# Transposed squares in a delta-rule inverse: a second product or a transpose of the copied square

## The chip, the cores and the metric

One core of one Trainium2 chip runs the whole kernel. The metric is the device time of one execution in microseconds, as the median of several runs. The core has TensorE (PE; its weight loads are listed as PEld), VectorE (DVE), ScalarE (ACT), GpSimd (POOL) and the DMA queues, one of them fed by SyncE (SP). They work side by side and wait for each other with semaphores.

## The reference, cut to what matters

The model is a two-layer trunk over 512 latent and 256 context tokens of width 1024. Each layer has three token mixers side by side (grouped attention, neighbourhood attention, a gated delta rule in both directions), a merge and an MLP. The change lies in the delta rule, where a 64 x 64 strictly triangular matrix per chunk and head is inverted by repeated squaring:

```
nil = jnp.where(strict, -jnp.einsum('nbhid,nbhjd->nbhij', kb, kc) * decay, 0.0)
tinv = jnp.eye(CHUNK, dtype=F32) + nil
power = nil
for _ in range(int(math.log2(CHUNK)) - 1):     # 5 times
    power = power @ power
    tinv = tinv + tinv @ power
w_v = tinv @ (vc * bc[..., None])
k_cd = tinv @ (kb * jnp.exp(gc)[..., None])
```

After this a scan over the chunks updates the state with w_v and k_cd. All of it is float32.

## The kernel before, in words

The program is written out by engine: `block.tensor`, `block.vector`, `block.scalar`, `block.gpsimd` and a SyncE part each hold one list of instructions, in program order, with waits between them. There is no planner; the order of the lines is the order on each engine.

**The delta stage.** Two chunks of 64 tokens stand on the diagonal of one 128 x 128 matrix, so a tile of 128 tokens is one step: `for s in range(TT)`, 6 steps per layer, 12 in all. Each step treats two directions (`d`, forward and backward, on different token tiles) and four heads (`h`), which lie beside each other in a 128 x 512 buffer. A step consists of the head (decays, L591 to L597; the matrix A, built by DVE up to L1264; its transpose AT, four PE transposes per direction, L604), five squaring iterations (`i`), then k_cd (L641) and two state updates (L656 to L674).

**One squaring iteration, before.** The stationary operand of a PE product is used transposed, so the kernel keeps the power and its transpose. `power(d, i)` names four buffers: `src`, `srcT` (the power and its transpose that come in) and `dst`, `dstT` (those that go out). They swap from one iteration to the next. For each direction PE multiplies, head by head, the square into columns 0 to 511 of a PSUM tile (L615) and, for i < 4, the transposed square into columns 512 to 1023 (L617). ACT copies the first half into `dst` (L953), DVE the second into `dstT` (L1275). Then PE multiplies `dst` with the transposed inverse `xbuf` (L626), and DVE adds the product to `xbuf` (L1279). The transposed square is needed only by the squares of the next iteration; at i = 4 there is none.

**PSUM.** There are four PSUM tiles `PS` of 128 x 1024. `take` hands them out in turn and waits until the tile's previous user has been read twice (its free count goes up by two). `read(...)` is that full count as a wait, `read_first(...)` the count less one, `full(...)` waits for PE's mark that the tile is filled, and `pair(...)` is the tile. `pe_done` is PE's own signal, with a named mark for each point.

**Between the iterations of layer 0.** For the first 20 iterations of layer 0 (steps 0 to 3, all five `i`), PE does one block of the modulation after each: `modulation_columns` (L407, one transpose) and `modulation` (L397, products with w_mod, four slots of 512 KB). The slots come through the ring `wring` of three, filled by SyncE's queue in the order of `plan` (L816); a slot's transfer is issued when PE has read the slot three before it. Steps 4 and 5 of layer 0 and all of layer 1 have nothing between the iterations.

**At the end of a step** POOL overwrites `pbuf` (L1517) once the last square (i = 4) is filled, and the head of the next step begins when the last state update of this one is read.

Of the kernel before, what the change touches and what calls it, by code (L numbers as in the profile page):

```python
# [21 lines left out]
P = 128  # L22
# [8 lines left out]
A_H, A_KV, B_H, C_H = 8, 2, 8, 4  # L31
# [71 lines left out]
def program(nc, a, out, x_store, skew, bias_rows, book):  # L103
    book["final"] = book.get("final", False)
    with ExitStack() as ctx:
# [35 lines left out]
        ident, ones, blk, rot = (cst[:, c:c + P] for c in (C_ID, C_ONE, C_BLK, C_ROT))  # L141
# [82 lines left out]
        act_done, dve_done, pool_done, pe_done = sig("act_done"), sig("dve_done"), sig("pool_done"), sig("pe_done")  # L224
# [14 lines left out]
        def full(*key):  # L239
            n = book.get(("ps",) + key, 0) if book["final"] else 0  # L240
            return ps_full[n % 4], n // 4 + 1
# [4 lines left out]
        def pair(*key):  # L246
            return PS[book.get(("ps",) + key, 0) % 4]
# [5 lines left out]
        def read(*key):  # L253
            n = book.get(("ps",) + key, 0) if book["final"] else 0
            return ps_free[n % 4], 2 * (n // 4 + 1)

        def read_first(*key):

            sem, n = read(*key)
            return sem, n - 1  # L260
# [111 lines left out]
        def _(pe):  # L372
            turn["n"] = 0
            mm, tr = nc.tensor.matmul, nc.tensor.transpose
# [144 lines left out]
            for l in range(DEPTH):  # L519
                if l == 0:  # L520

                    for t in range(TT):
                        pe.wait_ge(*x_in[t].at())
                        ps = take(pe, "x", t)
                        for k in range(KC):
                            last = tr(ps[:, k * P:k * P + P], r(S0 + 1024 * t, 1024)[:, k * P:k * P + P], ident)
# [15 lines left out]
                for p in range(15):  # L542
# [9 lines left out]
                    if p == 2:  # L552
                        pe.wait_ge(*read("baT", l))
                        ps = take(pe, "ba", l)
                        for t in range(TT):
                            last = tr(ps[:, 16 * t:16 * t + 16], baT[0:16, t * P:t * P + P], ident[0:16, 0:16])
                        last.then_inc(*filled("ba", l))
                    if p == 4:

                        pe.wait_ge(*dve_done.at("g", l))  # L560
                        ps = take(pe, "gc", l)
                        for t in range(TT):
# [4 lines left out]
                            for c in range(2):  # L567
                                last = mm(ps[:, b + 16 + 8 * c:b + 24 + 8 * c],
                                          blk[:, 64 * c:64 * c + 1].to_broadcast([P, P]), gt[:, t, :],
                                          start=True, stop=True)  # L570
                        last.then_inc(*filled("gc", l))
                    if p >= 3 and c_order[p - 3] < 8:
# [3 lines left out]
                        ps = take(pe, "css", l, j)  # L576
# [8 lines left out]
                for s in range(TT):  # L585
# [23 lines left out]
                    for i in range(5):  # L609
                        for d in range(2):  # L610
                            src, srcT, dst, dstT = power(d, i)
                            pe.wait_ge(*(read("pw", l, s, d, i - 1) if i else read("AT", l, s, d)))
                            ps = take(pe, "pw", l, s, d, i)
                            for h in range(C_H):
                                last = mm(ps[:, h * P:h * P + P], srcT[:, h, :], src[:, h, :], start=True, stop=True)  # L615
                                if i < 4:
                                    last = mm(ps[:, 512 + h * P:512 + h * P + P], src[:, h, :], srcT[:, h, :],  # L617
                                              start=True, stop=True)
                            last.then_inc(*filled("pw", l, s, d, i))
                        for d in range(2):  # L620
                            src, srcT, dst, dstT = power(d, i)
                            pe.wait_ge(*read("pw", l, s, d, i))
                            pe.wait_ge(*(read("X", l, s, d, i - 1) if i else read("AT", l, s, d)))
                            ps = take(pe, "X", l, s, d, i)
                            for h in range(C_H):
                                last = mm(ps[:, h * P:h * P + P], dst[:, h, :], xbuf[d][:, h, :], start=True, stop=True)  # L626
                            last.then_inc(*filled("X", l, s, d, i))
                        if l == 0:

                            if turned:  # L630
                                modulation_columns(*turned)
                            turned = next(filler, None)
                            if turned:
                                modulation(*turned)
# [421 lines left out]
        def _(dve):  # L1056
# [98 lines left out]
            for l in range(DEPTH):  # L1155
# [88 lines left out]
                for s in range(TT):  # L1244
                    for d in range(2):
                        t = tiles[d][s]
                        dve.wait_ge(*read_first("bc", l, s, d))
                        if s:
                            dve.wait_ge(*full("kcd", l, s - 1, d))
                        V.tensor_tensor(wbuf[d], pair("bc", l, s, d)[:, 0:512].rearrange("p (h n) -> p h n", h=C_H),  # L1250
                                        along(gcs[:, t, 4 * d:4 * d + 4]), ALU.subtract)\
                            .then_inc(*free("bc", l, s, d, by=1))
                        dve.wait_ge(*act_done.at("W", l, s, d))
                        dve.wait_ge(*full("G", l, s, d))
                        if s:
                            dve.wait_ge(*full("so", l, 2 * s - 1, d))
                        ps = pair("G", l, s, d)
                        V.tensor_tensor(flat(pbuf[d]), ps[:, 0:512], flat(wbuf[d]), ALU.mult)\
                            .then_inc(*free("G", l, s, d, by=1))
                        V.tensor_tensor(flat(aqbuf[d]), ps[:, 512:1024], flat(wbuf[d]), ALU.mult)\  # L1260
                            .then_inc(*free("G", l, s, d, by=1))
                        dve.wait_ge(*read("G", l, s, d))
                        dve.wait_ge(*pool_done.at("MB", l, s, d))
                        V.tensor_tensor(pbuf[d], pbuf[d], p2buf[d], ALU.mult).then_inc(*dve_done.mark("A", l, s, d))  # L1264
                    for d in range(2):
                        dve.wait_ge(*full("AT", l, s, d))
                        ps = pair("AT", l, s, d)
                        V.tensor_copy(flat(tbuf[d]), ps[:, 0:512]).then_inc(*free("AT", l, s, d, by=1))
                        V.tensor_tensor(xbuf[d], ps[:, 0:512].rearrange("p (h n) -> p h n", h=C_H), over_heads(ident),  # L1269
                                        ALU.add).then_inc(*free("AT", l, s, d, by=1))  # L1270
                    for i in range(5):
                        if i < 4:
                            for d in range(2):
                                dve.wait_ge(*full("pw", l, s, d, i))
                                V.tensor_copy(flat(power(d, i)[3]), pair("pw", l, s, d, i)[:, 512:1024])\  # L1275
                                    .then_inc(*free("pw", l, s, d, i, by=1))
                        for d in range(2):
                            dve.wait_ge(*full("X", l, s, d, i))
                            V.tensor_tensor(flat(xbuf[d]), pair("X", l, s, d, i)[:, 0:512], flat(xbuf[d]), ALU.add)\  # L1279
                                .then_inc(*free("X", l, s, d, i))  # L1280
                        if l == 0:
                            if turned:
                                modulation_columns(*turned)
                            turned = next(filler, None)
                            if turned:
                                modulation(*turned)
                    for c in range(2):
                        for d in range(2):
                            t, cc, n = tiles[d][s], (c if d == 0 else 1 - c), 2 * s + c
                            lo = 64 * cc  # L1290
                            ps = pair("so", l, n, d)
                            dve.wait_ge(*full("so", l, n, d))
                            if want_out(l, t):
                                o = Otok[lo:lo + 64, t, :]
                                if (t, cc) in seen:
                                    V.tensor_tensor(o, ps[lo:lo + 64, 512:1024], o, ALU.add).then_inc(*free("so", l, n, d, by=1))
                                else:
                                    V.tensor_copy(o, ps[lo:lo + 64, 512:1024]).then_inc(*free("so", l, n, d, by=1))
                                seen.add((t, cc))
                            dve.wait_ge(*pool_done.at("Sdec", l, n, d))  # L1300
                            S1 = state[:, (n + 1) % 2, 4 * d:4 * d + 4, :].rearrange("p a b -> p (a b)")
                            V.tensor_tensor(S1, ps[:, 0:512], S1, ALU.add)\
                                .then_inc(*free("so", l, n, d, by=1 if want_out(l, t) else 2))
# [338 lines left out]
```

## Time and profile before

| | |
|---|---|
| median of 3 runs | 3793.74 us (3784.53 to 3796.07) |
| profiled execution | 3801.55 us |
| its span on the core | 3799.7 us |
| its mean granted TensorE clock | 0.936 |
| TensorE busy | 3390.5 us (89%) |
| VectorE / ScalarE / GpSimd busy | 35% / 27% / 28% |
| squaring iterations (L615, L617, L626) busy on PE | 204.5, 171.4 and 126.8 us |

A span is from the first to the last instruction. Busy time counts the union of an engine's instructions; PE's overlap each other, so the mean duration of one is longer than the distance between two. One fp32 product shows as two MATMUL instructions, one fp32 transpose as one. "Granted clock" is the share of TensorE's full speed: 1.00 is 2.4 GHz, 0.50 is 1.2 GHz. In brackets behind an instruction stands how long its engine sat idle before it and whose work ended that.

### The profile page before, as it was taken

Reading aid. Unit: us, or ns where it says so; the run is one execution under the profiler, and the core shown is the slowest. Engines: PE = TensorE matmul, PEld = TensorE weight load, DVE = VectorE, ACT = ScalarE, POOL = GpSimd, SP = SyncE. Lnnn points to the kernel's source line nnn. Section 1 sums busy time; section 2 is a strip of 40 time slices with the busy share of each in tenths; the row PEclk is TensorE's granted clock in tenths of the full one; section 3 lists DMA queues with packets and bytes.
Section 4 is the critical chain, followed back from the end, with each engine's and each line's share of the span. In section 5 each row is a group of like instructions: output and inputs, shape, how many; then the busy total and the mean of one; then the engine's idle time right before and its main releaser. Section 6 shows DMA issues by size and latency. Waiting matters only on the chain.

```text
span 3799.7 us, 49641 instructions
## 1 busy us (share of the span) xinstructions
PE 3390.5 (89%) x21115; PEld 2809.3 (74%) x21115; DVE 1338.5 (35%) x1789; ACT 1014.4 (27%) x1614; POOL 1058.9 (28%) x679
## 2 busy tenths in 40 slices
PE   5977777989988999979999979799989989989997
PEld 3857777977766777858888858688977766658886
DVE  3672232412455111242222257544313552232222
ACT  2431111222354111232122133322222541133223
POOL 3232122232111111233223231333233022244443
PEclk6888899999999999989999988899999999989998
DMA  5213333011000222212222211000021013323331
GB/s 163 78 27 112 112 112 112 1 50 53 25 8 37 59 60 61 75 35 62 67 61 62 67 61 39 1 1 1 1 72 53 4 51 89 86 76 97 94 95 61
DMA packets 302570, 226.16 MB, mean 60 GB/s; under 512 B 16720, under 2 KB 275216, under 8 KB 301712
## 3 DMA queue, kind: packets, MB, share of 16 engines
q1 hardware_dynamic: 298992, 207.69, 18.6%
q0 software_dynamic: 3360, 15.29, 1.2%
q8 instruction: 169, 2.77, 0.3%
q14 instruction: 49, 0.40, 0.0%
HBM read 214.56 MB, written 9.36 MB: 59 GB/s over the span
## 4 chain that ended last, share of the span: by engine, by line
PE 81%; DVE 8%; DMA 3%; issue 3%; ACT 3%; POOL 1%; SPq 0%; ACTq 0%; POOLq 0%; DVEq 0%
PE ps L385 17%; PE ps L386 16%; PE ps L387 16%; PE ps L721 5%; PE ps L615 4%; PE ps L626 3%; DMA wring<-in_w_mod 3%; PE ps L617 3%; PE ps L465 2%; DVE stat L1100 1%; PE ps L486 1%; PE ps L669 1%; PE ps L512 1%; PE ps L656 1%; PE ps L503 1%
## 5 line engine op out<-in xcount | busy, mean ns | idle before, releaser
L385 PE MATMUL ps<-hh,wh 128*128 128x512 f32 (+1 forms) x2592 | 950.2, 367 | 106.9 <-DVE hl L1079 79.0
L1438 POOL TENSOR_TENSOR wl<-wring,wh 128x1024 fp32r<-128x1024 f32 x264 | 643.8, 2442 | 1379.4 <-ACT wh L867 1379.3
L386 PE MATMUL ps<-hl,wh 128*128 128x512 f32 (+1 forms) x2592 | 919.0, 355 | 0.0
L387 PE MATMUL ps<-hh,wl 128*128 128x512 f32 (+1 forms) x2592 | 917.7, 354 | 0.0
L385 PEld LDWEIGHTS ps<-hh,wh 128*128 128x128 f32 x2592 | 499.7, 193 | 202.8 <-issue 62.4
L386 PEld LDWEIGHTS ps<-hl,wh 128*128 128x128 f32 x2592 | 500.9, 193 | 74.0 <-issue 9.6
L387 PEld LDWEIGHTS ps<-hh,wl 128*128 128x128 f32 x2592 | 499.7, 193 | 67.6
L867 ACT ACTIVATE wh<-wring 128x1024 fp32r<-128x1024 f32 x264 | 277.6, 1054 | 909.4 <-DMA wring<-in_w_in 462.0
L386 PE MATMUL ps<-fl,wh 128*128 128x512 f32 (+1 forms) x768 | 274.8, 358 | 0.0
L387 PE MATMUL ps<-fh,wl 128*128 128x512 f32 (+1 forms) x768 | 274.5, 357 | 0.0
L385 PE MATMUL ps<-fh,wh 128*128 128x512 f32 (+1 forms) x768 | 274.3, 357 | 0.0
L1373 DVE SCALAR_TENSOR_TENSOR R<-ps,modcs,R 128x512 f32<-128x512 f32 x216 | 136.4, 659 | 389.7 <-PE ps L387 388.7
L721 PE MATMUL ps<-R,wring 128*128 128x512 f32 (+1 forms) x576 | 214.0, 521 | 0.0
L615 PE MATMUL ps<-R 128*128 128x128 f32 x960 | 204.5, 315 | 4.1 <-DVE R L1269 3.7
L1357 DVE TENSOR_TENSOR R<-ps,R 128x768 f32<-128x768 f32 (+1 forms) x48 | 39.6, 825 | 448.8 <-ACT R L1024 443.0
L1387 DVE TENSOR_TENSOR R<-R 128x768 f32<-128x768 f32 (+1 forms) x64 | 52.8, 826 | 367.0 <-ACT R L1041 367.0
L953 ACT ACTIVATE R<-ps 128x512 f32<-128x512 f32 x120 | 71.6, 597 | 401.1 <-PE ps L617 341.4
L615 PEld LDWEIGHTS ps<-R 128*128 128x128 f32 x960 | 167.4, 227 | 12.2 <-DVE R L1269 7.9
L617 PE MATMUL ps<-R 128*128 128x128 f32 x768 | 171.4, 310 | 0.0
L721 PEld LDWEIGHTS ps<-R,wring 128*128 128x128 f32 x576 | 107.5, 190 | 86.1 <-issue 80.5
L385 PEld LDWEIGHTS ps<-fh,wh 128*128 128x128 f32 x768 | 144.7, 188 | 23.7
L386 PEld LDWEIGHTS ps<-fl,wh 128*128 128x128 f32 x768 | 144.5, 188 | 23.3
(220 smaller groups left out, 4666.9 us busy)
## 6 DMA issues: line engine op xcount, KB each, us to landing
wring<-in_w_ffn SPq DMA_DIRECT2D x128, 512.0 KB, 4.0
wring<-in_w_in SPq DMA_DIRECT2D x116, 512.0 KB, 3.9
wring<-in_w_mod SPq DMA_DIRECT2D x96, 512.0 KB, 4.8
wring<-in_w_branch SPq DMA_DIRECT2D x48, 256.0 KB, 4.3
wring<-in_w_out SPq DMA_DIRECT2D x16, 512.0 KB, 4.0
x_store<-R POOLq DMA_DIRECT2D x2, 3072.0 KB, 9.6
R<-x_store POOLq DMA_DIRECT2D x2, 3072.0 KB, 10.8
R<-in_x SPq DMA_DIRECT2D x4, 512.0 KB, 7.5
```

What stands on the lines that cost most here:

```text
L385: mm(ps[:, t0:t1], ahk, rh[:, k, t0:t1], start=(k == 0), stop=False)
L386: mm(ps[:, t0:t1], ahk, rl[:, k, t0:t1], start=False, stop=False)
L387: last = mm(ps[:, t0:t1], alk, rh[:, k, t0:t1], start=False, stop=(k == kn - 1))
L465: last = mm(ps[u][:, c0:c0 + n1 - n0], q[lo:lo + HD, t * P:t * P + P], k[lo:lo + HD, n0:n1], start=True, stop=True)
L615: last = mm(ps[:, h * P:h * P + P], srcT[:, h, :], src[:, h, :], start=True, stop=True)
L617: last = mm(ps[:, 512 + h * P:512 + h * P + P], src[:, h, :], srcT[:, h, :], start=True, stop=True)
L626: last = mm(ps[:, h * P:h * P + P], dst[:, h, :], xbuf[d][:, h, :], start=True, stop=True)
L721: last = mm(ps[:, t0:t1], w[:, k, :], (oA, oB, oC)[x % 3][:, k, t0:t1], start=(k == 0), stop=(k == 3))
L867: A(slot_view(wh, n % NSPL, *slot), w, ACT.Copy).then_inc(*act_done.mark("whi", *slot))
L953: A(flat(power(d, i)[2]), pair("pw", l, s, d, i)[:, 0:512], ACT.Copy)\
L1373: V.scalar_tensor_tensor(out=xT[:, j, t0:t1], in0=pair(*key)[:, t0:t1], scalar=modc[:, gate + j, c:c + 1], in1=xT[:, j, t0:t1], op0=ALU.mu ...
L1438: G.tensor_tensor(slot_view(wl, n % NSPL, l, name, i), w, slot_view(wh, n % NSPL, l, name, i).bitcast(F32), ALU.subtract)\
```

## The change

PE no longer multiplies the transposed square (L617). Instead it waits until ACT has copied the square into `dst` (the first of the tile's two reads), transposes `dst` head by head into the same columns 512 to 1023 of the same PSUM tile, and marks that as `pwT`. DVE's copy into `dstT` waits for this mark, and DVE now goes direction by direction: transposed copy and X sum of direction 0, then those of direction 1. i = 4 is as before on PE and ACT. In this excerpt "..." stands for unchanged lines.

```diff
@@ PE: squares
                             for h in range(C_H):
                                 last = mm(ps[:, h * P:h * P + P], srcT[:, h, :], src[:, h, :], start=True, stop=True)
-                                if i < 4:
-                                    last = mm(ps[:, 512 + h * P:512 + h * P + P], src[:, h, :], srcT[:, h, :],
-                                              start=True, stop=True)
                             last.then_inc(*filled("pw", l, s, d, i))
                         for d in range(2):
                             src, srcT, dst, dstT = power(d, i)
-                            pe.wait_ge(*read("pw", l, s, d, i))
+                            if i < 4:
+
+                                pe.wait_ge(*read_first("pw", l, s, d, i))
+                                for h in range(C_H):
+                                    last = tr(pair("pw", l, s, d, i)[:, 512 + h * P:512 + h * P + P], dst[:, h, :], ident)
+                                last.then_inc(*pe_done.mark("pwT", l, s, d, i))
+                            else:
+                                pe.wait_ge(*read("pw", l, s, d, i))
                             pe.wait_ge(*(read("X", l, s, d, i - 1) if i else read("AT", l, s, d)))
...
@@ DVE: copies and sums
                     for i in range(5):
-                        if i < 4:
-                            for d in range(2):
-                                dve.wait_ge(*full("pw", l, s, d, i))
+                        for d in range(2):
+                            if i < 4:
+                                dve.wait_ge(*pe_done.at("pwT", l, s, d, i))
                                 V.tensor_copy(flat(power(d, i)[3]), pair("pw", l, s, d, i)[:, 512:1024])\
                                     .then_inc(*free("pw", l, s, d, i, by=1))
-                        for d in range(2):
                             dve.wait_ge(*full("X", l, s, d, i))
```

## Rows read from the trace of the kernel before

**Rows 1.** The page: span, and TensorE's busy time.
```profile
span 3799.7 us, 49641 instructions
PE 3390.5 (89%) x21115; PEld 2809.3 (74%) x21115; DVE 1338.5 (35%) x1789; ACT 1014.4 (27%) x1614; POOL 1058.9 (28%) x679
```

**Rows 2.** The page: the chain that ended last, by engine and by line.
```profile
PE 81%; DVE 8%; DMA 3%; issue 3%; ACT 3%; POOL 1%; SPq 0%; ACTq 0%; POOLq 0%; DVEq 0%
PE ps L385 17%; PE ps L386 16%; PE ps L387 16%; PE ps L721 5%; PE ps L615 4%; PE ps L626 3%; DMA wring<-in_w_mod 3%; PE ps L617 3%; PE ps L465 2%; DVE stat L1100 1%; PE ps L486 1%; PE ps L669 1%; PE ps L512 1%; PE ps L656 1%; PE ps L503 1%
```

**Rows 3.** Groups by line and shape: busy us, mean ns | idle before.
```profile
L615 PE MATMUL ps<-R 128*128 128x128 f32 x960 | 204.5, 315 | 4.1 <-DVE R L1269 3.7
```

**Rows 4.** Order of time, layer 1: start, us, engine, line, count.
```profile
2657.16 0.39 PE L615 MATMUL ps<-R 128*128 128x128 f32 x2
...
2660.74 2.10 PE L626 MATMUL ps<-R 128*128 128x128 f32 x16
2660.94 0.60 ACT L953 ACTIVATE R<-ps 128x512 f32<-128x512 f32 x1 [1.19 <-PE ps L617]
...
2662.68 0.39 PE L615 MATMUL ps<-R 128*128 128x128 f32 x2
```

**Rows 5.** Windows: stretch, length, busy by engine, clock, DMA share, GB/s.
```profile
2660.70:2666.20 5.50, 5.50 (x50) 5.42 (x50) 2.77 (x4) 1.19 (x2) 0.00 (x0) 1.00 0.00 0
2649.39:2653.80 4.41, 4.41 (x20) 4.41 (x21) 1.83 (x3) 0.60 (x1) 0.87 (x1) 0.50 0.00 0
```

**Rows 6.** Transposes: a group by line, and two runs in time.
```profile
L604 PE MATMUL ps<-cst,R 128*128 128x128 f32 x96 | 18.0, 317 | 43.9 <-DVE R L1264 43.9
...
14.46 1.09 PE L526 MATMUL ps<-cst,R 128*128 128x128 f32 x8 [0.24 <-DMA R<-in_ctx]
...
1103.84 1.53 PE L503 MATMUL ps<-cst,R 128*128 128x128 f32 x12
```

**Rows 7.** Order of time at i = 4, layer 1, step 4.
```profile
2673.71 1.95 PE L615 MATMUL ps<-R 128*128 128x128 f32 x16
...
2674.87 0.60 ACT L953 ACTIVATE R<-ps 128x512 f32<-128x512 f32 x1 [2.30 <-PE ps L615]
...
2675.52 2.05 PE L626 MATMUL ps<-R 128*128 128x128 f32 x16
```

**Rows 8.** Layer 0 around two modulations; the last two from the chain.
```profile
410.77 0.39 PE L626 MATMUL ps<-R 128*128 128x128 f32 x2
...
411.00 0.27 PE L407 MATMUL ps<-cst,mrow 128*128 128x128 f32 x1
...
411.20 1.52 PE L397 MATMUL ps<-wring,ccol 128*32 128x128 f32 x48
...
411.91 5.30 SPq L816 DMA_DIRECT2D wring<-in_w_mod  x4
...
415.69 1.08 PE L397 MATMUL ps<-wring,ccol 128*32 128x128 f32 x16 [2.98 <-DMA wring<-in_w_mod]
...
424.87 1.52 PE L397 MATMUL ps<-wring,ccol 128*32 128x128 f32 x48
...
481.47 1.94 PE ps L626 x16
...
492.45 1.94 PE ps L626 x16
```

**Rows 9.** Waits of TensorE, 279 to 760 us: total, times, longest.
```profile
PE ps L397 <- DMA wring<-in_w_mod: 62.6, 20, 4.5
```

**Rows 10.** Window over the steps with modulation; columns as in rows 5.
```profile
279.00:659.50 380.50, 301.90 (x3076) 275.46 (x3076) 109.13 (x193) 52.96 (x88) 80.89 (x73) 0.88 0.34 111
```

**Rows 11.** Windows over the first transposes, TensorE alone: busy, clock, DMA.
```profile
7.40:12.00 4.60, 4.60 (x22) 1.00 1.03 386
12.00:14.20 2.20, 2.20 (x20) 1.00 1.01 369
```

## The prediction

> **What bounds the kernel now.** I read the page's shares first, then the chain that ended last, the groups by line and shape, and last one squaring iteration in order of time. TensorE is busy for 3390.5 of 3799.7 us [rows 1]; the chain is TensorE for 81% of the span, and 4, 3 and 3% of it lie on L615, L617 and L626, the lines that the change touches [rows 2]. So what comes off TensorE here comes off the time, unless a wait takes its place.
>
> The stage is 12 steps (2 layers, 6 token tiles), each with 5 squaring iterations for two directions. The change touches i = 0 to 3, that is 48 iterations. In one of them in layer 1 [rows 4] TensorE issues 32 instructions for squares (L615, L617: each fp32 product shows as two) and 16 for X (L626). The squares start at 2657.16 and the next ones at 2662.68: 5.52 us for 48 instructions, while a window of 5.50 us shows TensorE busy throughout at granted clock 1.00 and VectorE for 2.77, ScalarE for 1.19 us [rows 5]. The durations of single instructions (315 ns in the mean) [rows 3] overlap and are not the price. The price is the distance of starts: 32 of them from 2657.16 to 2660.74, 0.112 each. 48 x 0.112 is 5.38; the remaining 0.14 lies inside L626 (16 instructions from 2660.74 to 2662.68, 1.94 instead of 1.79), where X of the second direction waits for the ScalarE copy that began at 2660.94.
>
> **The 16 squares that go.** Per iteration L617's 16 instructions go: 16 x 0.112 = 1.79 us.
>
> **The 8 transposes that come.** Transposes exist in the trace. A transpose is one instruction: L604 has 96, which is 12 steps x 2 directions x 4 heads [rows 6]. Spacing at full clock: 12 of them take 1.53 us with the last lasting 0.27, so (1.53 - 0.27)/11 = 0.115, a first restart included; 8 of L526 take 1.09, so 0.117 [rows 6].  I take 0.11. So 8 x 0.11 = 0.88. Bounds: 0.11 if they stream; 0.27 each (2.2 us) if each ran to its end before the next.
>
> **The new order and its waits.** Squares of direction 0 (8 instructions, 0.89), squares of 1 (to 1.79), then transposes of 0, which wait for ScalarE's copy of square 0. That hand-off is already in the trace, at i = 4, where there is no L617 [rows 7]: L615 starts at 2673.71, the copy at 2674.87 and takes 0.60, to 2675.47; L626 starts at 2675.52, 1.81 after the first square where 16 x 0.112 is 1.79. The wait costs 0.02 plus a restart of the array of about 0.1: 0.12, about the 0.14 that X of the second direction pays today and no longer will, because its transposes stand before it and come after the copy's end. In the new order, from the first square: transposes of 0 from 1.9 to 2.35, X of 0 to 3.25, transposes of 1 to 3.7 (copy 1 done at 1.99 + 0.60 = 2.6, no wait), X of 1 to 4.6. VectorE: transposed copy 0 from about 2.55 to 3.25, X sum 0 from 3.45 to 4.15, copy 1 from 4.15 to 4.85 (it is now queued behind X sum 0), X sum 1 from 4.85 to 5.5. The squares of direction 1 of the next iteration need copy 1 and come at 4.6 + 0.9 = 5.5: 0.6 us of slack, so VectorE hides; were that cover gone, TensorE would wait for it once per iteration. Squares of 0 need copy 0, done 1.3 us before. The PSUM tiles that the next iteration takes are free by the same times.
>
> New iteration: (16 + 16) x 0.112 + 0.88 + 0.12 = 4.58 against 5.52. Saving 0.94, in 32 iterations without anything between them (layer 0 steps 4 and 5, layer 1): 30.1 us. At each step's start the clock is low (granted 0.50 for 2649.39 to 2653.80 [rows 5]). If that low stretch keeps its length, what is removed is still paid at the full rate afterwards, so 0.94 stands for i = 0 too.
>
> **The 16 iterations with modulation between them** (layer 0, steps 0 to 3). Each ends in a product with w_mod through a ring of three slots; the fourth slot's transfer starts only when the first is read, and TensorE waits 3 us for it (2.98 [rows 8]; 62.6 us in 20 waits [rows 9]). That wait runs from the issue to the landing (411.91 to 415.69, 3.8 us), whatever the squares cost, and so it stays. The question is whether the other three slots are back in time. Four transfers are issued from 411.91 on, the last at 417.2, so by the same 3.8 us it lands at 421.0, 9.8 after the modulation began (411.20). The next begins at 424.87 today and at 423.9 with 0.94 less: covered. The quickest iteration took 11.0 (X groups at 481.47 and 492.45) and would take 10.0; the last to land is the third slot that it reads, which leaves it about 1 us. So 16 x 0.94 = 15.0. The modulation takes the PSUM tile that copy 1 frees; that is at 4.85, while it would start at 4.8: 0 to 0.2 us, taken 0.1, 1.6 in all. Then the clock: these iterations run at 0.88 granted over the stretch [rows 10], and their lengths go from 11.0 to 13.7 (411.20 to 424.87) by where the low stretches fall. The idle part, 3 us, becomes a larger share of a shorter iteration; I take 0.25 us more at the low level's cost for each, 4 us; either end is 1 us each way, 16 us.
>
> **The sum.** 30.1 + 15.0 - 1.6 - 4.0 = 39.5 us, say 40. The profiled execution took 3801.55 us around a span of 3799.7, so it would be 3762. It lies 7.8 above the median of the runs, 3793.74; from the median I get 3754.
>
> **Switching cost**, which no row shows for this pair of shapes exactly: there are four changes between full products and transposes in an iteration. From the last two L626 at 410.77 to the single transpose L407 at 411.00 are 0.23, no extra; from L407 to the narrow L397 takes 0.20, some 0.1 extra [rows 8]. Bounds 0 to 0.4 us an iteration, 19 us in all; I take 0, as both tiles here are 128 x 128 like L626 and L407.
>
> **A rule against it.** The first transposes of the kernel run with nothing else on TensorE: 22 instructions in the first 4.60 us (0.209 each, the 1.2 GHz level) and 20 in the next 2.20 us (0.110, the 2.4 GHz level) [rows 11] (the record of the clock begins later and its 1.00 says nothing of the first part). Transposes alone brought the clock up. The Trainium skill, "TensorE: Matmul & The Clock Gate", part 4 on PE-mode transpose, says that transpose mode does not count as busy for the clock and that one takes about 275 ns in a kernel's context. By that rule the changed iterations could fall to the lower level, the second rival below; the trace has the 273 ns as a duration and 0.11 as the spacing, and speaks against the first half.
>
> **Rivals.**
> 1. The ring takes back the gain of the 16 modulation iterations, by a later landing or a worse fall of the low stretches: only the 32 others pay, 30 us, 3764. For it: the margin of about 1 us in the quickest iteration. Against: the 3.9 us between landing and use in the iteration of rows 8.
> 2. Slower: the clock. The place is the squaring iterations, now with 0.88 of 4.58 us in transposes and a restart in each. If the 32 iterations ran at 1.2 GHz they would take 9.2 instead of 5.5 us, 32 x 3.6 = 117 slower, 3911. It decides from 80 us of additional low clock, each microsecond of which loses half of one. Against: rows 11, and attention, where 12 transposes stand in each unit at the full rate [rows 6].
> 3. Slower: transposes cost their own 0.273 in sequence: 8 x 0.16 = 1.3 more, 0.36 slower an iteration, 17 us, 3811. Against: the spacing of every row of transposes.
> 4. Each switch costs 0.1: 48 x 0.4 less, gain 21, 3773.
> 5. The ScalarE hand-off is exposed where the i = 4 row shows it hidden (0.60 + 0.2 us): 0.15 remains of an iteration, 7 us, 3787, no difference. The change would then not shorten the chain, only exchange products for a wait.
>
> **Chances.** Forecast 0.73, rival 1 0.12, rival 4 0.07, rival 5 0.03, rival 2 0.03, rival 3 0.02. 0.3%, 11.4 us, is what can be told from no change. Faster 0.92, same 0.03, slower 0.05. The range: at the good end 45 us and 10 from a better fall of the clock, 3738; at the other rival 4, 3773; I leave out rivals 2, 3 and 5. 3736 to 3774.
>
> **What would show it.** Right: L615 x960 and 384 transposes with spacing 0.11; X groups 4.6 us apart in layer 1 at granted 1.00; transposes of direction 0 starting 1.8 to 1.9 after the first square; VectorE's copy 1 ending before squares of direction 1; the modulation wait still 3 us; nothing else moved. Wrong: X groups further apart than 4.8; idle before L615 behind VectorE's copy; a granted clock under 0.90 in steps without modulation; waits on w_mod that grow by what the squares lose.

## The result and the profile after

The changed kernel took 3741.27 us in the median of 4 runs (3737.76 to 3744.07), the kernel before 3789.47 in 4 runs beside it: ratio 0.9871, 95% interval 0.9851 to 0.9892, so 48 us or 1.3% less. Timed again in five rounds (experiment 1) the ratio was 0.9847 (0.9826 to 0.9867), which is 1.5% or some 58 us; the two intervals overlap. Forecast were 3754 and a gain of 40.

The page of the profiled execution (3744.07 us), beside [rows 1, 2]: span, busy time, the chain by line (X is now L630, the transposes are L623).

```profile
span 3742.2 us, 48873 instructions
PE 3332.5 (89%) x20731; PEld 2755.2 (74%) x20731; DVE 1334.2 (36%) x1789; ACT 1014.9 (27%) x1614; POOL 1059.7 (28%) x679
PE 81%; DVE 8%; DMA 3%; issue 3%; ACT 3%; POOL 1%; SPq 0%; ACTq 0%; POOLq 0%; DVEq 0%
PE ps L385 17%; PE ps L386 17%; PE ps L387 17%; PE ps L725 6%; PE ps L615 4%; PE ps L630 3%; DMA wring<-in_w_mod 3%; DVE stat L1104 2%; PE ps L465 2%; PE ps L486 1%; PE ps L673 1%; PE ps L512 1%; PE ps L623 1%; PE ps L660 1%; PE ps L503 1%
```

TensorE has 384 instructions fewer (768 of L617 out, 384 transposes in) and 58.0 us less busy time, about what the span lost (57.5), and its share in the chain is still 81%. The other engines do what they did. L617's 3% of the chain have become 1% of L623.

One full iteration of layer 1 in order of time, beside [rows 4]: start, duration, engine, line, count; in brackets the idle time before.

```profile
2608.62 1.95 PE L615 MATMUL ps<-R 128*128 128x128 f32 x16
...
2609.71 0.60 ACT L957 ACTIVATE R<-ps 128x512 f32<-128x512 f32 x1 [3.58 <-PE ps L615]
2610.36 0.42 PEld L623 LDWEIGHTS ps<-cst,R 128*128 128x128 f32 x4
2610.41 0.61 PE L623 MATMUL ps<-cst,R 128*128 128x128 f32 x4
...
2610.86 1.06 PE L630 MATMUL ps<-R 128*128 128x128 f32 x8
2611.05 0.69 DVE L1279 COPY R<-ps 128x512 f32<-128x512 f32 x1 [1.47 <-PE ps L623]
...
2611.75 0.60 PE L623 MATMUL ps<-cst,R 128*128 128x128 f32 x4
2612.02 0.69 DVE L1282 TENSOR_TENSOR R<-ps,R 128x512 f32<-128x512 f32 x1 [0.27 <-PE ps L630]
...
2612.18 1.06 PE L630 MATMUL ps<-R 128*128 128x128 f32 x8
2612.63 0.68 DVE L1279 COPY R<-ps 128x512 f32<-128x512 f32 x1
...
2613.08 0.28 PE L615 MATMUL ps<-R 128*128 128x128 f32 x1
```

Read the starts: 2608.62 to 2613.08 is 4.46 us, where [rows 4] had 5.52. The squares take 1.79 (to 2610.41), four transposes 0.45 (to 2610.86, the last 0.11 of it their step to the product), and nowhere is there a gap. ScalarE's copy ends at 2610.31, the load of the first transpose begins 0.05 later, and the transpose itself starts 0.11 after the last square, as if there had been no wait. 1.06 is saved where the prediction had 0.94: of the 0.12 that it charged for the hand-off only about 0.01 came (0.45 for four transposes, where 4 x 0.109 is 0.44). VectorE's second copy ends at 2613.31; the squares of direction 1 that need it start at 2613.08 + 0.89 = 2613.97, the 0.6 us of slack that was forecast.

Three stretches, before and after: modulation iterations (layer 0, steps 0 to 3), the rest of layer 0's stage, layer 1's stage. Columns: stretch, length, busy time of PE, PEld, DVE, ACT, POOL, granted clock, DMA share, GB/s. First the kernel before:

```profile
279.06:659.46 380.40, 301.86 (x3076) 275.42 (x3076) 109.03 (x192) 52.96 (x88) 80.79 (x73) 0.88 0.34 111
659.46:750.79 91.33, 87.56 (x687) 83.68 (x688) 39.30 (x59) 19.84 (x34) 25.07 (x23) 0.94 0.00 1
2419.07:2739.06 319.99, 297.82 (x2334) 281.48 (x2335) 137.53 (x202) 72.80 (x122) 105.33 (x95) 0.95 0.00 1
```

and the changed one:

```profile
279.44:646.58 367.14, 290.33 (x2947) 263.05 (x2947) 107.47 (x192) 52.98 (x88) 80.81 (x73) 0.86 0.35 115
646.58:728.19 81.61, 77.73 (x623) 74.31 (x624) 38.53 (x59) 19.84 (x34) 25.09 (x23) 0.95 0.01 1
2392.50:2683.60 291.10, 269.40 (x2142) 254.85 (x2143) 135.29 (x202) 72.85 (x122) 105.45 (x95) 0.95 0.00 1
```

The stage gave 13.3 + 9.7 + 28.9 = 51.9 us; the remaining 5.6 of the two spans lie outside it, where nothing was changed, and are within the scatter of single executions (the five-round runs of before go from 3784 to 3805). Between the two layers' stages the first profile of the changed kernel took 1664.3 us and its second 1668.0, with no edit between them; the two of before took 1668.3 and 1668.1. The clock in the steps without modulation is 0.95 in both stretches (before: 0.94 and 0.95); in the modulation stretch it is 0.86 instead of 0.88.

### The profile page after: what moved, and what is told of

Read it like the earlier page. It is cut to its first block, busy times and chain, and to the rows that moved or that the text cites. A ratio compares the mean times of both kernels' runs of the same rounds, so it can differ in the third digit from the quotient of the medians.

```text
span 3742.2 us, 48873 instructions
## 1 busy us (share of the span) xinstructions
PE 3332.5 (89%) x20731; PEld 2755.2 (74%) x20731; DVE 1334.2 (36%) x1789; ACT 1014.9 (27%) x1614; POOL 1059.7 (28%) x679
## 3 DMA queue, kind: packets, MB, share of 16 engines
q1 hardware_dynamic: 298992, 207.69, 18.5%
## 4 chain that ended last, share of the span: by engine, by line
PE 81%; DVE 8%; DMA 3%; issue 3%; ACT 3%; POOL 1%; SPq 0%; ACTq 0%; POOLq 0%; DVEq 0%
PE ps L385 17%; PE ps L386 17%; PE ps L387 17%; PE ps L725 6%; PE ps L615 4%; PE ps L630 3%; DMA wring<-in_w_mod 3%; DVE stat L1104 2%; PE ps L465 2%; PE ps L486 1%; PE ps L673 1%; PE ps L512 1%; PE ps L623 1%; PE ps L660 1%; PE ps L503 1%
## 5 line engine op out<-in xcount | busy, mean ns | idle before, releaser
L385 PEld LDWEIGHTS ps<-hh,wh 128*128 128x128 f32 x2592 | 498.9, 192 | 202.9 <-issue 62.6
L387 PEld LDWEIGHTS ps<-fh,wl 128*128 128x128 f32 x768 | 144.4, 188 | 23.3
L615 PE MATMUL ps<-R 128*128 128x128 f32 x960 | 156.4, 331 | 3.7 <-DVE R L1273 3.1
L615 PEld LDWEIGHTS ps<-R 128*128 128x128 f32 x960 | 146.9, 242 | 13.1 <-DVE R L1273 7.6
```

Of the source, the lines that this page charges most:

```text
L385: mm(ps[:, t0:t1], ahk, rh[:, k, t0:t1], start=(k == 0), stop=False)
L387: last = mm(ps[:, t0:t1], alk, rh[:, k, t0:t1], start=False, stop=(k == kn - 1))
```

## The experiments

**1. The changed kernel again** (after_again), no edit.

> The changed kernel, unedited, for a narrower ratio and a second profile. Theory: an iteration without modulation again takes 4.46 us (32 product instructions at 0.112 and 8 transposes at 0.109), in all 32 places. What the first iteration of a step loses to the low clock (0.9 to 2.5 us in the first profile after, 1.1 to 3.0 before) should come out differently per step, but with the same sum of 12 to 15 us over the 8 steps without modulation, if the shorter step causes it; if it was the luck of one profile, nearer to the 19 us of before. Time 3737 to 3745, ratio 0.987 to 0.988.

Measured: 3738.96 us, ratio 0.9847 (0.9826 to 0.9867). All 24 iterations with i = 1 to 3 outside the modulation take 4.46 (one 4.54). The 8 first iterations of a step take 16.2 us more than 8 x 4.46; in the first profile after it was 14.0. So my bound of 12 to 15 was missed, and that loss scatters by some 2 us. The three stretches are 368.4, 83.0 and 291.9 us.

**2. The kernel before again** (before_again), no edit.

> The kernel before, unedited, for a second profile of the first iterations of the 8 steps without modulation. If its loss there is a property of the order of work, it is again 18 to 19 us (three steps of layer 1 at 8.5 us each); if it was chance, it lies anywhere between 12 and 19.

Measured: 3800.67 us in its one timed run; stretches 381.3, 90.8 and 320.0. The loss of the first iterations is 18.3, after 18.9 in the first profile. In layer 1 they repeat to 0.01 us: 8.56, 8.55, 8.54 in its first three steps the first time and 8.57, 8.55, 8.54 now; in layer 0 they differ (7.87 and 8.14, now 7.53 and 7.96). So for this kernel the loss is no luck of one profile. The changed kernel does not repeat in this way: its first iterations in the same three steps took 5.75, 6.97 and 5.97 in the first profile and 7.51, 6.25 and 5.60 in the second.

**3. Same products, squares first** (products_after). In the kernel before (VectorE's transposed copy then waits for `pwT`):

```diff
                             for h in range(C_H):
                                 last = mm(ps[:, h * P:h * P + P], srcT[:, h, :], src[:, h, :], start=True, stop=True)
-                                if i < 4:
-                                    last = mm(ps[:, 512 + h * P:512 + h * P + P], src[:, h, :], srcT[:, h, :],
-                                              start=True, stop=True)
                             last.then_inc(*filled("pw", l, s, d, i))
+                        for d in range(2 if i < 4 else 0):
+                            src, srcT, dst, dstT = power(d, i)
+                            for h in range(C_H):
+                                last = mm(pair("pw", l, s, d, i)[:, 512 + h * P:512 + h * P + P], src[:, h, :], srcT[:, h, :],
+                                          start=True, stop=True)
+                            last.then_inc(*pe_done.mark("pwT", l, s, d, i))
```

> The kernel before with one move: the squares of both directions first, then the transposed squares of both as products, then X; VectorE waits for the second group. Same instructions as before. Theory A (number of instructions): an iteration takes 48 x 0.112 = 5.37 us, so only the 0.14 restart of X in direction 1 goes; 48 x 0.14 = 7 us under before, 3783. Rival B (the order is what pays, since ScalarE's copy gets a head start): most of the 48 us come here too, 3745 to 3760. Rival C (nothing): the restart stays because X waits for both copies; 5.5, within 3 us of before.

Measured: ratio 1.0001 (0.9988 to 1.0014), 5.52 us an iteration. Theory A's 7 us did not come, and not the rival's 48 either: rival C was right. Its iteration (squares L615, second products L620, X L629):

```profile
2661.10 1.95 PE L615 MATMUL ps<-R 128*128 128x128 f32 x16
...
2662.20 0.60 ACT L956 ACTIVATE R<-ps 128x512 f32<-128x512 f32 x1 [4.46 <-PE ps L615]
2662.89 1.95 PE L620 MATMUL ps<-R 128*128 128x128 f32 x16
...
2663.99 0.69 DVE L1278 COPY R<-ps 128x512 f32<-128x512 f32 x1 [1.92 <-PE ps L620]
2664.73 2.05 PE L629 MATMUL ps<-R 128*128 128x128 f32 x16
```

ScalarE's copy ends at 2662.80, two microseconds before X. X starts at 2664.73, 0.05 after the end of VectorE's copy of the transposed square (2664.68). X waits with `read("pw", ...)`, the full count of the tile, that is for both copies, though it uses only ScalarE's. The same holds in the kernel before, and there the two end close together: ScalarE's at 2660.94 + 0.60 = 2661.54 [rows 4], VectorE's at 2660.94 + 0.69 = 2661.63:

```profile
2660.94 0.69 DVE L1275 COPY R<-ps 128x512 f32<-128x512 f32 x1 [1.09 <-PE ps L617]
```

I had put that wait down to ScalarE. It gave a new theory, F, and the next two kernels.

**4. Before, with X waiting for ScalarE alone** (x_waits_act). VectorE's copy now waits for ScalarE's, so that the first read of the tile is ScalarE's for certain:

```diff
-                            pe.wait_ge(*read("pw", l, s, d, i))
+                            pe.wait_ge(*(read_first("pw", l, s, d, i) if i < 4 else read("pw", l, s, d, i)))
...
-                                dve.wait_ge(*full("pw", l, s, d, i))
+                                dve.wait_ge(*read_first("pw", l, s, d, i))
```

> The kernel before with one wait changed: VectorE copies the transposed square only after ScalarE's copy of the square, and X waits for ScalarE's copy alone (in the kernel before X waits for both copies). Theory F: the 0.14 restart in each iteration of before came from VectorE's copy, which takes 0.69 us where ScalarE's takes 0.60, not from ScalarE's as the prediction had it; without it an iteration takes 5.37 to 5.45 instead of 5.52, 3 to 7 us faster than before. Rival: the restart comes from ScalarE's copy; 5.52 stays and the time is that of before.

Measured: ratio 0.9979 (0.9968 to 0.9989), 5.42 us an iteration (X groups of this kernel at 2650.09 and 2655.51). Theory F holds: 0.10 of the 0.14 was VectorE's copy. The gain in time, 0.2%, is small beside the scatter of single executions; the iteration's length is the surer sign.

```profile
2650.09 2.01 PE L626 MATMUL ps<-R 128*128 128x128 f32 x16
...
2655.51 2.01 PE L626 MATMUL ps<-R 128*128 128x128 f32 x16
```

**5. Both edits of 3 and 4** (products_after_x). VectorE's copy waits for the second group and for ScalarE's copy.

> products_after (squares of both directions, then both transposed squares as products, then X), and X waits for ScalarE's copy alone. products_after stayed at 5.52 us, because X waited there for VectorE's copies. Theory F: now every wait is over long before, so 48 x 0.112 = 5.37 us an iteration, 7 us under before, and the rest of the changed kernel's 1.06 us (0.92) belongs to the number of instructions alone. Rival: it stays at 5.52 again, and the restart is the cost of a switch from one group of products to the next.

Measured: ratio 0.9970 (0.9959 to 0.9981), 5.36 us an iteration. Squares, second products and X follow at 1.79, 1.79 and 1.78 us, no gap and no restart:

```profile
2643.01 1.95 PE L615 MATMUL ps<-R 128*128 128x128 f32 x16
2644.80 1.95 PE L620 MATMUL ps<-R 128*128 128x128 f32 x16
2646.59 1.95 PE L629 MATMUL ps<-R 128*128 128x128 f32 x16
2648.37 0.83 PE L615 MATMUL ps<-R 128*128 128x128 f32 x6
```

This is the kernel before without its wait: the same 48 product instructions. Against 5.52 the waits of before cost 0.16 an iteration. What the changed kernel has beyond it, 5.36 - 4.46 = 0.90, is products against transposes alone.

**6. Products in the transposes' place** (product_in_place). In the changed kernel:

```diff
-                                    last = tr(pair("pw", l, s, d, i)[:, 512 + h * P:512 + h * P + P], dst[:, h, :], ident)
+                                    last = mm(pair("pw", l, s, d, i)[:, 512 + h * P:512 + h * P + P], src[:, h, :], srcT[:, h, :],
+                                              start=True, stop=True)
```

> The changed kernel, but at the place of the four transposes stand the four products of the transposed square (8 instructions), behind the same wait for ScalarE's copy. Theory A: 48 x 0.112 = 5.37 plus a restart of 0.12 at the wait, since a product has two weight loads where a transpose has one: 5.49 us an iteration, 1 to 7 us under before. Rival B (the place and the wait matter, not what is done there): as fast as the changed kernel, 4.5 us.

Measured: ratio 0.9981 (0.9966 to 0.9997), 5.42 us an iteration. The rival, that place and wait are what pays, falls. My restart of 0.12 was too much again; it is 0.06, all in the first group after the wait:

```profile
2697.95 1.95 PE L615 MATMUL ps<-R 128*128 128x128 f32 x16
2699.74 1.12 PE L623 MATMUL ps<-R 128*128 128x128 f32 x8
2700.69 1.06 PE L631 MATMUL ps<-R 128*128 128x128 f32 x8
2701.58 1.06 PE L623 MATMUL ps<-R 128*128 128x128 f32 x8
2702.47 1.06 PE L631 MATMUL ps<-R 128*128 128x128 f32 x8
2703.37 0.39 PE L615 MATMUL ps<-R 128*128 128x128 f32 x2
```

The first L623 group takes 0.95 from its start to the next group, the second 0.89. The profiled execution took 3773.03, the shortest of this kernel's ten and 17 us under their median, so its stretch with modulation is not typical.

**7. Every transpose twice** (double_tr). In the changed kernel:

```diff
-                                for h in range(C_H):
+                                for h in list(range(C_H)) * 2:
                                     last = tr(pair("pw", l, s, d, i)[:, 512 + h * P:512 + h * P + P], dst[:, h, :], ident)
```

> The changed kernel with every transpose of a square done twice into the same columns. Theory A (a transpose costs its spacing): 8 x 0.109 = 0.87 more, 5.33 us an iteration, 48 x 0.87 = 42 over the changed kernel, near 3783. Rival D (a transpose costs its duration, 0.27): the spacing is 0.27 and 2.2 us come on top, 105 us. Rival E (transposes don't hold the clock up): the granted clock in steps without modulation falls from 0.95 towards 0.8 and the time is over 3800; by theory A it stays.

Measured: 3780.19 us, ratio 0.9963 (0.9944 to 0.9982), 41 above the changed kernel run beside it (42 expected). An iteration takes 5.34:

```profile
2641.82 1.95 PE L615 MATMUL ps<-R 128*128 128x128 f32 x16
2643.61 1.05 PE L623 MATMUL ps<-cst,R 128*128 128x128 f32 x8
2644.50 1.06 PE L630 MATMUL ps<-R 128*128 128x128 f32 x8
2645.39 1.04 PE L623 MATMUL ps<-cst,R 128*128 128x128 f32 x8
2646.26 1.06 PE L630 MATMUL ps<-R 128*128 128x128 f32 x8
2647.16 0.39 PE L615 MATMUL ps<-R 128*128 128x128 f32 x2
```

8 x 0.109 = 0.87 more: a transpose costs its spacing and not its duration. With a third of the iteration in transposes (1.75 of 5.34 us), TensorE spends 26.4 us of layer 1's stage at the low clock. The changed kernel has 26.4 and 30.1 in its two profiles, the kernels with products alone 29.8 to 30.1 (experiments 4, 5 and 6) and 33.5 (before, twice, and experiment 3). The granted clock is 1.00 over the iteration shown, and over that of the changed kernel from 2608.62 to 2613.08. The Trainium skill ("TensorE: Matmul & The Clock Gate", PE-mode transpose) says that transpose mode does not count as busy for the clock in the same way. The trace shows nothing of it in a stream of which 33% are transposes, nor did [rows 11] for transposes alone.

**8. VectorE's old order** (old_dve_order). In the changed kernel:

```diff
-                        for d in range(2):
-                            if i < 4:
+                        if i < 4:
+                            for d in range(2):
                                 dve.wait_ge(*pe_done.at("pwT", l, s, d, i))
                                 V.tensor_copy(flat(power(d, i)[3]), pair("pw", l, s, d, i)[:, 512:1024])\
                                     .then_inc(*free("pw", l, s, d, i, by=1))
+                        for d in range(2):
```

> The changed kernel with VectorE's order of before: both transposed copies, then both X sums. Theory A: in steps without modulation VectorE has 0.6 us of slack either way, so an iteration stays at 4.46. After a modulation iteration the PSUM tile that modulation takes comes free 0.25 us sooner, so TensorE's 15 short waits for VectorE's copy before L397 (3.7 us in sum on the weight loads) go: 0 to 4 us faster than the changed kernel. Rival: the new order on VectorE is what keeps the squares fed, and undoing it costs 0.2 us or more an iteration, 10 us slower.

Measured: 3737.62 us, ratio 0.9846 (0.9831 to 0.9862), the iteration at 4.46. It can't be told from the changed kernel (0.9847). TensorE's 15 short waits for VectorE's copy, which by the theory were to go, shrank only from 3.7 us to 2.5. This half of the edit is free either way; the rival falls.

**9. What is left in the stage: modulation spread out** (spread_mod). In the changed kernel `modulation` gets the slots to do, and a block is spread over one iteration:

```diff
-            def modulation(l, cb):
-                ps = take(pe, "mod", l, cb)
-                for kk in range(4):
+            def modulation(l, cb, kks=(0, 1, 2, 3)):
+                ps = take(pe, "mod", l, cb) if kks[0] == 0 else pair("mod", l, cb)
+                for kk in kks:
...
+                        block = next(filler, None) if l == 0 else None
+                        if block:
+                            modulation(*block, (0,))
                         for d in range(2):
...
                             last.then_inc(*filled("X", l, s, d, i))
+                            if block and d == 0:
+                                modulation(*block, (1,))
+                        if block:
+                            modulation(*block, (2,))
                         if l == 0:
...
-                            turned = next(filler, None)
+                            turned = block
                             if turned:
-                                modulation(*turned)
+                                modulation(*turned, (3,))
```

> The changed kernel with the four slots of a modulation block taken at four points of one squaring iteration (after the squares, after X of direction 0, after X of direction 1, at the end) instead of all at the end. Theory: what is left in these 20 iterations is the 3 us wait for the fourth slot (60.6 us in 20 waits) and the low clock that follows it (some 100 us of low clock in the stretch, half of it lost). Spread, TensorE works while a slot is on its way: an iteration needs 4.46 + 4 x 0.45 = 6.3 us of work, and 2.1 MB at the 380 GB/s that the queue reached need 5.5. Expected 6.5 to 9 us instead of 12, 60 to 100 us under the changed kernel, 3640 to 3680. Rival: the transfers are bound by the three slots, each read freeing one that is back 4.5 us later; then each of the four points waits about 1 us and the iteration stays near 10.5, only 25 us faster.

Measured: 3679.67 us (3678.0 to 3681.58), ratio 0.9692 (0.9677 to 0.9707). An iteration with modulation:

```profile
440.90 2.02 PE L616 MATMUL ps<-R 128*128 128x128 f32 x16 [0.56 <-DVE mrow L1141]
443.24 0.64 PE L397 MATMUL ps<-wring,ccol 128*32 128x128 f32 x16 [0.31 <-DMA wring<-in_w_mod]
443.81 0.66 PE L627 MATMUL ps<-cst,R 128*128 128x128 f32 x4
444.30 1.06 PE L634 MATMUL ps<-R 128*128 128x128 f32 x8
445.29 0.64 PE L397 MATMUL ps<-wring,ccol 128*32 128x128 f32 x16
445.87 0.65 PE L627 MATMUL ps<-cst,R 128*128 128x128 f32 x4
446.36 1.06 PE L634 MATMUL ps<-R 128*128 128x128 f32 x8
447.34 0.65 PE L397 MATMUL ps<-wring,ccol 128*32 128x128 f32 x16
447.92 0.33 PE L408 MATMUL ps<-cst,mrow 128*128 128x128 f32 x1
448.18 0.64 PE L397 MATMUL ps<-wring,ccol 128*32 128x128 f32 x16
```

Most of these iterations take 8.1 to 8.7 us (the longest 10.2) instead of 10.2 to 13.5. TensorE's waits for w_mod fell from 60.6 us in 20 to 7.6 in 14, and the stretch from 367.1 to 306.0 at a granted clock of 0.95:

```profile
278.06:584.06 306.00, 272.05 (x2947) 233.73 (x2947) 110.94 (x193) 52.98 (x88) 80.70 (x73) 0.95 0.45 138
```

The new wait is in the first row above: the next squares stand behind VectorE's copy of the modulation, since they take the next PSUM tile in turn (8.4 us in 15 waits).

**10. The same with VectorE's old order** (spread_mod_dve); the edit is that of 8 on top of 9.

> spread_mod with VectorE's order of before. In the spread iterations VectorE has more to do between the squares; by the theory the order costs and gains nothing, within 3 us of spread_mod.

Measured: 3675.74 us (3673.01 to 3680.3), ratio 0.9684 (0.9668 to 0.9700); 3.9 under spread_mod, within overlapping intervals, so the two can't be told apart. Its median is the lowest of all, 121 us under before.

## Why the prediction was right, point by point

| part of the gain, us | predicted | measured |
|---|---|---|
| 16 product instructions out, 8 transposes in, per iteration | 1.79 - 0.88 = 0.91 | 0.90 (5 against the changed kernel) |
| waits, per iteration | 0.02 | 0.16 (before against 5) |
| 32 iterations without modulation | 30.1 | 33.9 |
| the first iterations' loss to the low clock | 0 | 3.5 |
| 16 iterations with modulation | 9.4 | 13.1 |
| the stage | 39.5 | 50.3 |

The measured column is the mean of the two profiles of each kernel: stage 791.9 against 741.6. The stage came out 11 us better than forecast: 3.8 in the 32 iterations, 3.5 in the first iterations, 3.7 in those with modulation. The 3.8 is explained by experiments, and so is 16 x 0.12 = 1.9 of the 3.7. The rest goes with where the low clock falls, and no experiment separates it.

- **What bounds**: right. TensorE lost only 0.16 us of an iteration to waits, and what left it left the time.
- **The price of a product and of a transpose by spacing**: right to 0.01 us an iteration, and shown by taking each alone (experiments 5 and 7). Rival 3, the duration of 0.27, and rival 4, a cost at each switch, fall: the step from a transpose to a product is 0.11.
- **The hand-off from ScalarE**: right that it is hidden, wrong in its price, and this is the term of the sum that was mis-sized: 0.12 charged, 0.01 measured. I took the 0.12 from i = 4 [rows 7]. There a product waits, and the copy ended 0.03 before it was due (2675.47 against 2673.71 + 1.79 = 2675.50). In the changed kernel a transpose waits and the copy ended 0.10 before it was due (2610.31 against 2610.41). A product in that place, with the same 0.10 (2699.64 against 2699.74), pays 0.06 (experiment 6). So by these rows both differences count; the copy's lead was not varied alone. Rival 5 falls.
- **The wait that goes**: its size in the sum was right, since the 0.14 was counted as gone, and with the restart it goes whole (0.16 by experiment 5). Its reading was wrong. I read [rows 4] as X waiting for ScalarE's copy, and set this off against the new wait for the same copy, so that only 0.02 was left. It was waiting for VectorE's copy of the transposed square, which X does not use (experiments 3 and 4), and the changed kernel no longer waits for that; the new wait was no equal of it. Together the two make 0.12 of an iteration; 32 x 0.12 = 3.8 us.
- **The first iterations**: I expected their loss to the low clock to stay. It went from 18.6 (18.9, 18.3) to 15.1 (14.0, 16.2). These 3.5 us I had put at nothing, so as far as the prediction goes they were luck. Transposes are not needed for it: 4, 5 and 6 have only products and lose 14.3, 15.2 and 13.8. Only the kernels with 5.52 us an iteration lose 18 (before twice, experiment 3: 18.5). Why just these fall so badly stays open.
- **The modulation iterations**: the wait stayed (62.6 to 60.6 us in 20), so rival 1 did not happen. (The last of the four transfers is issued at 416.84; the 417.2 of the prediction is the end of that issue, so the margin was 0.4 larger than it said.) Of 16 x 1.06 = 17.0 us 13.1 came. The low clock in the stretch went from 94 us (93.7, 94.6) to 103 (100.9, 105.6); half of the 9 us more is 4.6, near the 4.0 that I had taken. 17.0 - 4.6 = 12.4 leaves nothing for the 1.6 that I had charged for the PSUM tile. The clock is the part that no edit alone tells apart: experiment 6 spent 70 us of the stretch at the low level, experiment 4 104 us, for the same iteration of 5.42.
- **Rival 2, the clock** falls with experiment 7, and with the granted 1.00 over an iteration of the changed kernel.
- **Against the profile's own time** I had 3762, and that execution took 3744: 12.4 us more from the stage (51.9 against 39.5), and 5.6 outside the stage that are scatter.

## What to carry to other kernels

Price TensorE instructions by the distance of their starts in a full stream; an fp32 transpose of 128 x 128 then costs 0.109 us where the product costs 0.224, so a transposed copy of a result that exists is worth taking from a transpose, where the wait for that result is covered as it is here. When an instruction waits for a count that two engines raise, work out the end of both before naming the one that holds it. And where a stage's filler work waits for a ring of buffers, spreading its slots between the other work can be worth as much as cheaper arithmetic: here 59 us more, by the ratios of experiments 1 and 9, after the 58 of the change.

## What was not expected of the hardware

- How the restart after a semaphore depends on how late it comes and on what waits. Products behind a copy that ended 0 to 0.03 us before they were due lost 0.12 to 0.14 us [rows 4, 7]. Behind one that ended 0.10 before, they lost 0.06 (experiment 6) and transposes 0.01 (the first starts 1.79 us after the first square, which is 16 x 0.112). In each case the first load began only some 0.05 us after the copy's end. The loads are 0.14 us for a transpose and 0.19 for a product; that this is the reason was not tested alone.
- The loss to the low clock at the start of a step repeated to 0.01 us in layer 1 between two executions of the kernel before, but not between two of the changed kernel, where single iterations moved by up to 1.8 us (5.75 and 7.51). Over the 8 steps it is 18 to 19 us at 5.52 us an iteration and 13 to 16 at the shorter ones, 5.42 among them.
